# Feed-forward weight products as seven half-size products each (Strassen's scheme), inner width in parts of 6, 8 and 8 tiles

## The chip, the cores and the metric

The kernel runs on one core of a Trainium2 chip. The metric is the time of one execution on the device in microseconds. The names of the engines are those of the profile: PE multiplies matrices (PEld is its weight load), DVE and ACT work on elements from SBUF and PSUM, POOL works on elements in SBUF, SP issues the DMAs. R is the row of reciprocal root mean squares of a normalization, one number per token.

## What is computed

Two transformer blocks, one behind the other, on 512 tokens of width 1024, all in float32. The change concerns the feed-forward part that ends each block:

```python
D_FF = 2816
h = h + mixed @ w_out
hn = rms_norm(h, ffn_norm_g)
h = h + (silu(hn @ w_ffn_gate) * (hn @ w_ffn_up)) @ w_ffn_down
```

Everything else (projections, four kinds of attention, gates, branch products) stays as it is.

## The kernel before

Activations stand transposed: `hT` holds the residual as 8 tiles of 128 features by 512 tokens. Every float32 product is made of three fast ones: a matrix is split into a high part (a rounded copy in the type fp32r) and a low part (what the copy leaves), and PE adds high x high, high x low and low x high in PSUM. ACT makes the high part of the weights (`high`, L605, `stage` to `wh`), DVE the low part (`low`, L904, `wl`), or POOL in the phases named in `POOL_LOW` (L516). The weights of a product are one tile of 128 outputs: 8 or 11 blocks of 128x128, 1024 or 1408 columns in `stage`, in two slots. `product` (L1529) runs over the blocks k and the three parts, 24 or 33 matmuls of 512 tokens each into one bank of `psL`.

The feed-forward part is cut into two halves of the inner width, 11 tiles each (`NFH`): phases gu1a, dn1a, gu1b, dn1b for the first layer and the same with 2. A pair of gu is one tile of gate and one of up. For each pair DVE multiplies both products by R (L1313, L1319), ACT takes the tanh (L790), DVE makes the hidden value (L1317, L1321), ACT and DVE split it (L794, L1323) into `hid`. A pair of dn is two of the 8 output chunks, which DVE adds to `hT` (L1338). ACT and DVE also do the squares and gains of the next normalization beside dn1b and dn2b, and beside `out_project`, the phase before.

The order on each engine is written by hand. Engines meet at semaphores: `w_in` (weights landed), `hi`, `lo`, `mm` (product done), `ev` (PSUM bank read). PE goes on as soon as the low part of the next tile is there and its bank is free:

```python
pe.wait_ge(lo[b], PAIR0[name] + i + 1)
pe.wait_ge(ev[b], PAIR0[name] + i)
```

## Time and profile before

| | us |
|---|---|
| median of 2 runs | 1661.76 (1650.31 to 1673.21) |
| the profiled execution | 1652.3 |
| its span, first to last instruction | 1650.5 |
| PE busy | 1607.5 (97%) |
| DVE busy | 839.7 (51%) |
| ACT busy | 535.2 (32%) |
| POOL busy | 203.8 (12%) |

The span leaves 1.8 us of the execution's time outside. Busy PE is the union of its matmuls, which overlap: the time from the start of one to the start of the next is what a stream of them costs, not the duration of one. For DVE, ACT and POOL the mean duration of one operation is also about what it costs in a queue.

### The profile page before, as it was taken

How to read it: one execution, taken by the hardware profiler on the slowest of the kernel's cores; microseconds unless marked ns; L12 is line 12 of the kernel's file. 1: busy time of each engine (PE TensorE's matmuls, PEld its weight loads, DVE VectorE, ACT ScalarE, POOL GpSimd, SP SyncE). 2: the span in 40 equal slices, each digit the busy share in tenths (PEclk: the TensorE clock that was granted, in tenths of full speed). 3: DMA queues.
4: the chain of work that ended last, by engine and by line, in shares of the span. 5: the costliest groups of instructions: out<-in, count | busy, mean ns of one | idle time of the engine just before them, and what ended most of it. 6: DMA issues, size and time to landing. Idle time of an engine off the chain costs nothing.

```text
span 1650.5 us, 21586 instructions
## 1 busy us (share of the span) xinstructions
PE 1607.5 (97%) x7698; PEld 1273.5 (77%) x7698; DVE 839.7 (51%) x1579; ACT 535.2 (32%) x978; POOL 203.8 (12%) x140
## 2 busy tenths in 40 slices
PE   7899999999999999999999999999999999999997
PEld 6766776777878888888899777677777888888886
DVE  5277796436555533555554382332465554245543
ACT  4123443433322322223321363443333322122232
POOL 2222221003000000000002372221220000000000
PEclk9999999999999999999999999999999999999999
DMA  5832220003333332333232201111133333323331
GB/s 142 204 106 60 57 65 20 1 14 107 90 90 102 99 105 77 89 98 104 81 87 78 62 14 52 52 42 36 51 102 98 94 89 109 94 77 99 95 105 69
DMA packets 250508, 132.62 MB, mean 80 GB/s; under 512 B 20938, under 2 KB 247366, under 8 KB 250447
## 3 DMA queue, kind: packets, MB, share of 16 engines
q1 hardware_dynamic: 248318, 123.92, 26.5%
q0 software_dynamic: 2048, 7.77, 1.8%
q8 instruction: 37, 0.61, 0.2%
q14 instruction: 25, 0.20, 0.0%
q10 hardware_dynamic: 80, 0.14, 0.0%
HBM read 129.67 MB, written 6.38 MB: 82 GB/s over the span
## 4 chain that ended last, share of the span: by engine, by line
PE 91%; DVE 5%; DMA 2%; issue 1%; ACT 1%; POOL 0%; SPq 0%; DVEq 0%; ACTq 0%
PE psL L1529 59%; PE psL L1652 12%; PE psS L1529 4%; PE psL L1773 2%; PE psS L1902 2%; PE psT L1663 2%; PE psS L1703 1%; PE psS L1751 1%; DMA stage<-in_w_in 1%; PE psS L1717 1%; PE psL L1868 1%; PE psS L1885 1%; DMA xin<-in_x 1%; DVE W L1158 1%; PE psT L1666 1%
## 5 line engine op out<-in xcount | busy, mean ns | idle before, releaser
L1529 PE MATMUL psL<-hn,wh 128*128 128x512 f32 x1664 | 525.4, 397 | 5.2 <-POOL wl L516 5.0
L1529 PEld LDWEIGHTS psL<-hn,wh 128*128 128x128 f32 x1664 | 313.1, 189 | 82.6 <-POOL wl L516 5.2
L605 ACT ACTIVATE wh<-stage 128x1024 fp32r<-128x1024 f32 (+3 forms) x234 | 239.8, 1025 | 308.8 <-PE psL L1529 199.4
L1529 PE MATMUL psL<-hn,wl 128*128 128x512 f32 x832 | 329.8, 396 | 0.0
L904 DVE TENSOR_TENSOR wl<-stage,wh 128x1024 fp32r<-128x1024 f32 (+1 forms) x152 | 198.8, 1308 | 95.2 <-ACT wh L605 90.3
L1529 PE MATMUL psL<-hid,wh 128*128 128x512 f32 x704 | 221.3, 395 | 0.0
L516 POOL TENSOR_TENSOR wl<-stage,wh 128x1024 fp32r<-128x1024 f32 (+2 forms) x82 | 156.1, 1904 | 522.6 <-ACT wh L605 522.6
L1529 PEld LDWEIGHTS psL<-hn,wl 128*128 128x128 f32 x832 | 156.8, 188 | 36.5
L1652 PE MATMUL psL<-hn,wh 128*128 128x512 f32 x512 | 173.0, 419 | 0.0
L1529 PEld LDWEIGHTS psL<-hid,wh 128*128 128x128 f32 x704 | 132.3, 188 | 32.0
L1529 PE MATMUL psL<-hid,wl 128*128 128x512 f32 x352 | 139.2, 396 | 0.0
L1652 PEld LDWEIGHTS psL<-hn,wh 128*128 128x128 f32 x512 | 87.4, 189 | 35.7 <-issue 22.1
L1652 PE MATMUL psL<-hn,wl 128*128 128x512 f32 x256 | 101.1, 395 | 0.0
L794 ACT ACTIVATE hid<-ft 128x512 f32 (+1 forms) x44 | 27.8, 632 | 208.6 <-DVE ft L1321 208.6
L1529 PE MATMUL psS<-hn,wh 128*128 128x264 f32 x448 | 86.3, 294 | 0.7 <-DVE hn L949 0.7
L1529 PE MATMUL psL<-mix,wh 128*128 128x512 f32 x256 | 80.7, 396 | 0.9 <-DVE wl L904 0.9
L1338 DVE TENSOR_TENSOR hT<-hT,psL 128x512 f32 (+1 forms) x32 | 22.0, 688 | 112.5 <-PE psL L1529 112.5
L1529 PEld LDWEIGHTS psL<-hid,wl 128*128 128x128 f32 x352 | 66.1, 188 | 16.0
L1158 DVE CUSTOM_DVE_ANT_0 W3b<-psS,biasW,sinkb 128x272 f32<-128x272 f32 (+1 forms) x32 | 18.1, 567 | 112.1 <-PE psS L1885 82.6
L790 ACT ACTIVATE ft<-ft 128x512 f32<-128x512 f32 x44 | 27.8, 632 | 146.0 <-DVE ft L1313 146.0
L1529 PEld LDWEIGHTS psS<-hn,wh 128*128 128x128 f32 x448 | 71.8, 194 | 2.5 <-issue 1.2
L1529 PE MATMUL psS<-hn,wl 128*128 128x264 f32 x224 | 64.8, 289 | 0.0
(356 smaller groups left out, 2038.0 us busy)
## 6 DMA issues: line engine op xcount, KB each, us to landing
stage<-in_w_in SPq DMA_DIRECT2D x54, 512.0 KB, 3.8
stage<-in_w_ffn_gate SPq DMA_DIRECT2D x22, 512.0 KB, 3.8
stage<-in_w_ffn_up SPq DMA_DIRECT2D x22, 512.0 KB, 3.8
stage<-in_w_ffn_down SPq DMA_DIRECT2D x16, 704.0 KB, 4.5
stage<-in_w_ff_gate SPq DMA_DIRECT2D x22, 512.0 KB, 3.8
stage<-in_w_ff_up SPq DMA_DIRECT2D x22, 512.0 KB, 3.8
stage<-in_w_ff_down SPq DMA_DIRECT2D x16, 704.0 KB, 4.6
stage<-in_w_out SPq DMA_DIRECT2D x16, 512.0 KB, 3.8
```

Source lines behind the costliest of these rows:

```text
L516: pool.tensor_tensor(wl[:, b, 0:n], stage[:, b, 0:n], wh[:, b, 0:n].bitcast(F32), ALU.subtract).then_inc(lo[b], 1)
L605: act.activation(wh[:, b, 0:n], stage[:, b, 0:n], ACT.Copy).then_inc(hi[b], 1)
L790: act.activation(ft[:, 1, :], ft[:, 0, :], ACT.Tanh, scale=0.5).then_inc(t_ok, 1)
L794: act.activation(hid[:, 0, bass.ds(i, 1), :], ft[:, 4, :], ACT.Copy).then_inc(hid_hi, 1)
L904: v.tensor_tensor(wl[:, b, 0:n], stage[:, b, 0:n], wh[:, b, 0:n].bitcast(F32), ALU.subtract).then_inc(lo[b], 1)
L1158: dv.link(v.tensor_tensor_reduce(out=tile, in0=scores, in1=bias, scale=1.0, scalar=least, op0=ALU.add, op1=ALU.max, accum_out=mx[:, col:co ...
L1338: v.tensor_tensor(hT[:, n, :], hT[:, n, :], psL[:, b, :], ALU.add).then_inc(ev[b], 1)
L1529: ins = pe.matmul(dst, w[:, b, k * P:(k + 1) * P], x[:, part, k, c0:c1], start=k + n == 0, stop=k == kc - 1 and n == 2)
L1652: ins = pe.matmul(psL[:, b, :], w[:, b, k * P:(k + 1) * P], hn[:, part_, k, META:], start=k + n == 0, stop=k == KD - 1 and n == 2)
L1663: ins = pe.transpose(psT[:, 0, n * P:(n + 1) * P], tile[:, col:col + P], ident[:])
L1773: ins = pe.matmul(psL[:, 0, 0:P], cn[0:w, c, :], pt, start=n == 0, stop=n == len(parts) - 1)
L1902: ins = pe.matmul(psS[:, 2 * (i % 2) + 1, h * HD:(h + 1) * HD], pt, vbn[0:w, c, h // 4 * HD:h // 4 * HD + HD], start=n == 0, stop=n == len ...
```

## The change

A pair of weight tiles is now one block product by Strassen's scheme (the form with 15 additions). For gate and up: the left factor has two tiles (gate, up) and two halves of the contraction, the right one two halves of the contraction and two halves of the tokens. In place of eight half products there are seven, each with 128 outputs, 256 tokens and 4 blocks of contraction (3 in the down products of the first part): matmuls of 256 columns, 84 (63) per pair. Down products pair two output chunks (0 with 4, and so on, `CHUNKS`).

Weights: POOL makes four sums of the quarters (`ffn_weights`: s3, s2, s4, s1, each of half a tile's columns); ACT makes high parts (`ffn_high`: 0 of one quarter, 1 and 2 of two sums each, 3 of two quarters); DVE makes the low parts (`ffn_low_a`, `ffn_low` 1 and 2, `ffn_low_aa`). They lie in seven slots in `wh`, `whx`, `wl`, `wlx`; `stagex` is a second buffer for a pair of weights.

Right factors: seven blocks per pair of tiles in `xb` (normalized input) and `hb` (hidden values). DVE makes three instructions of sums (`x_sums`), ACT the high parts, DVE the low ones.

Outputs: products 0, 2 and 4 grow in one PSUM bank; ACT copies it after each of them (`pa`, `pu`, `pv`), and PE may start product 2 or 4 only behind the copy before (`f_copy`). DVE adds the copies to products 1, 3, 5 and 6. Product 6 uses product 1's bank, so PE waits for DVE's first right quarter (`f_add`). R is read from PSUM. The low parts of `out1` and `out2` go from DVE to POOL. The inner width is cut in three parts of 6, 8 and 8 tiles.

The core of the diff:

```diff
-POOL_LOW = ("iq1", "aq1", "uq1", "gates1", "br1", "qa2", "qb2", "gates2", "br2")
+POOL_LOW = ("iq1", "aq1", "uq1", "gates1", "br1", "out1", "qa2", "qb2", "gates2", "br2", "out2")
+CHUNKS = [0, 4, 1, 5, 2, 6, 3, 7]
+SUBS = [(0, 6), (6, 8), (14, 8)]
...
+                for pair in layer_pairs(l):
+                    f0, n = SUBS[pair.sub]
+                    if pair.q % NQ >= 2:
+                        sp.wait_ge(faa_lo, pair.q - 1)
...
+            def ffn_weights(pair):
...
+                raw_here(pair)
+                slot_free(pair, 1)
+                pool.tensor_tensor(s3, a11, a21, ALU.subtract).then_inc(f_sum, 1)
+                slot_free(pair, 2)
+                pool.wait_ge(f_sum, 4 * q + 1)
+                pool.tensor_tensor(s2, a22, s3, ALU.subtract).then_inc(f_sum, 1)
+                slot_free(pair, 3)
+                pool.wait_ge(f_sum, 4 * q + 2)
+                pool.tensor_tensor(s4, a12, s2, ALU.subtract).then_inc(f_sum, 1)
+                slot_free(pair, 4)
+                pool.tensor_tensor(s1, a21, a22, ALU.add).then_inc(f_sum, 1)
...
+            def slot_free(pair, j):
+                if not pair.first:
+                    pool.wait_ge(f_prod, 7 * (pair.q - 1) + j + 1)
...
+            def ffn_low(pair, n):
+                v.wait_ge(f_sum, 4 * pair.q + 2 + n)
+                v.wait_ge(f_hi, 4 * pair.q + n + 1)
...
+            def gate_up(pair, head=None):
...
+                if pair.i:
+                    hidden(prev, slice(0, SEQ), 0)
+                ffn_low_aa(pair)
+                if odd:
+                    for n in range(3):
+                        x_sums(build, c, n)
+                    x_low(build, hb, c, 0)
...
+                ffn_low_a(nxt)
+                ffn_low(nxt, 1)
+                right_quarters(pair)
+                if odd:
+                    x_low(build, hb, c, 1)
...
+                ffn_low(nxt, 2)
...
+                upper_left(pair)
...
+                gated(pair, LEFT if pair.last else slice(0, SEQ), 3)
...
+                lower_left(pair)
...
+            def down(pair, after=None):
...
+                right_quarters(pair)
+                if nxt:
+                    ffn_low(nxt, 2)
+                upper_left(pair)
+                scaled_in(pair, o0, 2 * pair.i, 3)
+                lower_left(pair)
+                scaled_in(pair, o1, 2 * pair.i + 1, 4)
...
+                        if j in (2, 4):
+                            pe.wait_ge(f_copy, 3 * q + j // 2)
+                        if j in (3, 5):
...
+                                pe.wait_ge(f_add, 4 * (q - 1) + (2 if j == 3 else 3))
+                        if j == 6:
+                            pe.wait_ge(f_add, 4 * q + 1)
...
+                            for n, (wt, part) in enumerate(((high_slot(j, w), 0), (high_slot(j, w), 1), (low_slot(j, w), 0))):
+                                ins = pe.matmul(z_bank(pair, j), wt[:, c * P:(c + 1) * P], x[:, part, c, BLK[j], :],
```

What stands in a row on DVE before, the last gate/up pair of the first half (`ft` and `hid` are the steps of the hidden value, names in brackets the semaphores):

```order
L904 TENSOR_TENSOR wl<-stage,wh 128x1024 [waits hi1]
L1313 TENSOR_TENSOR ft<-psL,Rk 128x512 [waits mm0]
L904 TENSOR_TENSOR wl<-stage,wh 128x1408 [waits hi0]
L1317 SCALAR_TENSOR_TENSOR ft<-ft 128x512 [waits t_ok]
L1319 TENSOR_TENSOR ft<-psL,Rk 128x512 [waits mm1,dve_own]
L1321 SCALAR_TENSOR_TENSOR ft<-ft 128x512 [waits ev1]
L1323 TENSOR_TENSOR hid<-ft,hid 128x512 [waits hid_hi]
```

And now, the third gate/up pair of the first part, one of those with sums of hidden blocks (`wlx<-wsx,whx` and `wl<-ws,wh` are the lows of the next pair's sums, `ux` and `gx` the up and gate values):

```order
L1560 TENSOR_TENSOR wl<-stagex,wh 128x1024 [waits f_hi]
L1522 TENSOR_TENSOR xq<-xq 128x2x256 [waits xq_ok]
L1525 TENSOR_TENSOR xq<-xq 128x256 [waits x_sum]
L1530 TENSOR_TENSOR xq<-xq 128x256 [waits x_sum]
L1535 TENSOR_TENSOR hb<-xq,hb 128x512 [waits x_hi]
L1554 TENSOR_TENSOR wlx<-stage,whx 128x512 [waits f_hi]
L1549 TENSOR_TENSOR wlx<-wsx,whx 128x1024 [waits f_hi,f_sum]
L1624 TENSOR_TENSOR ux<-pv,psS 128x256 [waits f_copy,xq_ok]
L1625 TENSOR_TENSOR gx<-pv,psL 128x256
L1537 TENSOR_TENSOR hb<-xq,hb 128x1280 [waits x_hi]
L1549 TENSOR_TENSOR wl<-ws,wh 128x1024 [waits f_hi,f_sum]
L1630 TENSOR_TENSOR gx<-pa,psL 128x256 [waits f_prod]
```

The upper left quarter of this pair (L1630) now stands behind the low of the next pair's last two sums (L1549), which waits for ACT and through it for POOL.

ACT before, a gate/up pair of the first half:

```order
L605 ACTIVATE wh<-stage 128x1024 [waits mm1,w_in1]
L790 ACTIVATE ft<-ft 128x512 [waits ev0]
L605 ACTIVATE wh<-stage 128x1408 [waits mm0,w_in0]
L794 ACTIVATE hid<-ft 128x512 [waits hid_ok]
```

ACT now, from the copy behind product 0 of an ordinary pair to that of the next (`psT<-gx` is the tanh):

```order
L1035 ACTIVATE pa<-psS 128x256 [waits f_add,f_prod]
L956 ACTIVATE whx<-stagex 128x512 [waits f_prod,raw_in00]
L1048 ACTIVATE pu<-psS 128x256 [waits f_add,f_prod]
L960 ACTIVATE whx<-wsx 128x1024 [waits f_prod,f_sum]
L1056 ACTIVATE pv<-psS 128x256 [waits f_add,f_prod]
L960 ACTIVATE wh<-ws 128x1024 [waits f_prod,f_sum]
L1022 ACTIVATE psT<-gx 128x512 [waits gx_ok]
L958 ACTIVATE wh<-stagex 128x1024 [waits f_prod,raw_in01,raw_in00]
L1035 ACTIVATE pa<-psS 128x256 [waits f_add,f_prod]
```

The copy that lets PE into product 2 of the next pair (the last row) stands behind the tanh of this pair and the high of the next pair's last two blocks.

## Rows read from the trace of the kernel before

**Rows 1.** The page: busy time of each engine, and the chain by engine.
```profile
PE 1607.5 (97%) x7698; PEld 1273.5 (77%) x7698; DVE 839.7 (51%) x1579; ACT 535.2 (32%) x978; POOL 203.8 (12%) x140
...
PE 91%; DVE 5%; DMA 2%; issue 1%; ACT 1%; POOL 0%; SPq 0%; DVEq 0%; ACTq 0%
```

**Rows 2.** By stage: span, busy (xcount) of PE, PEld, DVE, ACT, POOL; clock, DMA, GB/s.
```profile
467.60:826.00 358.40, 358.38 (x1539) 288.98 (x1540) 175.77 (x199) 102.13 (x124) 0.00 (x0) 1.00 0.33 94
1278.60:1637.00 358.40, 358.37 (x1539) 288.96 (x1540) 165.73 (x190) 96.68 (x115) 0.00 (x0) 1.00 0.31 90
```

**Rows 3.** The chain in order of time: start us, us, what.
```profile
467.62 358.32 PE psL L1529 x1536
...
839.69 49.38 PE psS L1529 x405
```

**Rows 4.** DVE by form: xcount | busy us, mean ns | idle before.
```profile
L904 DVE TENSOR_TENSOR wl<-stage,wh 128x1024 fp32r<-128x1024 f32 x120 | 146.9, 1224 | 72.2 <-ACT wh L605 67.3
L904 DVE TENSOR_TENSOR wl<-stage,wh 128x1408 fp32r<-128x1408 f32 x32 | 51.9, 1623 | 23.0 <-ACT wh L605 23.0
L1321 DVE SCALAR_TENSOR_TENSOR ft<-ft 128x512 f32<-128x512 f32 x44 | 30.5, 692 | 1.5
...
L1252 DVE TENSOR_TENSOR mix<-mix 128x512 f32<-128x512 f32 x16 | 25.1, 1568 | 1.7
...
L1234 DVE COPY lat<-psL 128x128 f32<-128x128 f32 x32 | 9.3, 292 | 34.9 <-PE psL L1773 34.8
...
L1272 DVE SCALAR_TENSOR_TENSOR hn<-hT,gvec,hn x12 | 9.0, 752 | 16.3 <-ACT hn L770 16.3
```

**Rows 5.** ACT by form.
```profile
L605 ACT ACTIVATE wh<-stage 128x1024 fp32r<-128x1024 f32 x166 | 174.2, 1050 | 194.0 <-PE psL L1529 84.7 <-PE psS L1529 69.2 <-PE psL L1652 20.1
...
L790 ACT ACTIVATE ft<-ft 128x512 f32<-128x512 f32 x44 | 27.8, 632 | 146.0 <-DVE ft L1313 146.0
...
L718 ACT ACTIVATE PTb<-psT 128x256 f32<-128x256 f32 x16 | 5.7, 357 | 0.0
```

**Rows 6.** POOL by form.
```profile
L516 POOL TENSOR_TENSOR wl<-stage,wh 128x1024 fp32r<-128x1024 f32 x46 | 110.6, 2406 | 332.6 <-ACT wh L605 332.6
L516 POOL TENSOR_TENSOR wl<-stage,wh 128x512 fp32r<-128x512 f32 x32 | 42.6, 1331 | 172.8 <-ACT wh L605 172.8
...
L516 POOL TENSOR_TENSOR wl<-stage,wh 128x256 fp32r<-128x256 f32 x4 | 2.9, 731 | 17.2 <-ACT wh L605 17.2
```

**Rows 7.** Timeline of branch products 1: start us, us, engine, line.
```profile
375.71 1.29 POOL L516 TENSOR_TENSOR wl<-stage,wh 128x512 fp32r<-128x512 f32 x1 [1.01 <-ACT wh L605]
375.85 1.70 DVE L1252 TENSOR_TENSOR mix<-mix 128x512 f32<-128x512 f32 x1
...
377.67 0.63 ACT L758 ACTIVATE mix<-mix 128x512 f32 x1 [2.04 <-DVE mix L1252]
...
378.21 0.62 ACT L605 ACTIVATE wh<-stage 128x512 fp32r<-128x512 f32 x1
...
378.46 0.69 DVE L1254 TENSOR_TENSOR mix<-mix,mix 128x512 f32 x1 [0.91 <-ACT mix L758]
...
378.90 1.40 POOL L516 TENSOR_TENSOR wl<-stage,wh 128x512 fp32r<-128x512 f32 x1 [1.90 <-ACT wh L605]
379.07 0.68 DVE L1244 SCALAR_TENSOR_TENSOR mix<-gate,psL 128x512 f32<-128x512 f32 x1
```

**Rows 8.** Timeline in the index stage, DVE and POOL.
```profile
96.28 2.40 POOL L516 TENSOR_TENSOR wl<-stage,wh 128x1024 fp32r<-128x1024 f32 x1 [4.63 <-ACT wh L605]
...
96.45 2.58 DVE L1085 TENSOR_TENSOR ikx<-ikn,st 128x320 f32<-128x320 f32 x1
...
99.07 0.49 DVE L1086 TENSOR_TENSOR tmp<-ikx 128x320 f32<-128x320 f32 x1
```

**Rows 9.** Timeline of DVE in gates 1, two operations in a row.
```profile
206.25 0.69 DVE L1141 TENSOR_TENSOR tmp<-psL,Rk 128x512 f32<-128x512 f32 x1
206.85 0.16 DVE L1170 TENSOR_TENSOR st<-st,rsum 128x8 f32<-128x8 f32 x1
```

More of the change, by code:

```diff
@@ L250, in build @@
         assert o <= top[0]
+        spare = keep("spare", [P, 2304])
         hn0 = top[0]
@@ new lines, in build, with scratch, raw, high_slot @@
+        ux2, o = at("ux2", [P, SEQ], o)
+        pa2, o = at("pa2", [P, HALF], o)
+        pu2, o = at("pu2", [P, HALF], o)
+        pv2, o = at("pv2", [P, HALF], o)
+        assert o <= hn0
+        def scratch(pair):
+            return (gx2, ux2, pa2, pu2, pv2) if pair.kind == "dn" and pair.sub == 2 else (gx, ux, pa, pu, pv)
+        def raw(pair, m, part):
+            return (stage if pair.par else stagex)[:, m, part * pair.half:(part + 1) * pair.half]
+        def high_slot(j, width):
+            return whx[:, j, 0:width] if j < 3 else wh[:, (j - 3) // 2, (j - 3) % 2 * SEQ:(j - 3) % 2 * SEQ + width]
@@ L330, in build, with raw_blocks @@
+        def raw_blocks(group):
+            return blocks(xq, tuple(g + (g > 4) for g in group))
         hgf, _ = at("hgf", [P, KD, SEQ], hn0)
@@ L589, in _ @@
             lows("br2")
+            lows("out2")
+            for pair in layer_pairs(2):
+                ffn_weights(pair)
         @block.scalar
@@ L819, in pair1, with ffn_high @@
-            def pair1(i, last):
-                high(name, i, 1)
-                chunk1(i, 0)
-                high_next(name, i, last)
-                chunk1(i, 1)
-            act.wait_ge(mm[1], PAIR0[name])
-            act.activation(hn[:, 0, :, 0:META], metaT[:, 1, :, :], ACT.Copy).then_inc(mhi, 1)
-            with act.Fori(0, PAIRS[name] - 1) as i:
-                pair1(i, False)
-            pair1(PAIRS[name] - 1, True)
+            def ffn_high(pair, n):
+                q, w = pair.q, pair.half
+                if n in (0, 3):
+                    for m in range(1 if n == 0 else 2):
+                        act.wait_ge(raw_in[pair.par][m], 16 * (q // 2 + 1))
+                else:
+                    act.wait_ge(f_sum, 4 * q + 2 * n)
+                if not pair.first:
+                    act.wait_ge(f_prod, 7 * (q - 1) + (1, 3, 5, 7)[n])
+                elif n >= 2:
+                    act.wait_ge(mm[n - 2], PAIR0[f"out{pair.layer}"] + PAIRS[f"out{pair.layer}"])
+                if n == 0:
+                    act.activation(high_slot(0, w), raw(pair, 0, 0), ACT.Copy).then_inc(f_hi, 1)
+                elif n == 3:
+                    act.activation(two_slots(wh, 5, w), (stage if pair.par else stagex)[:, :, w:2 * w], ACT.Copy).then_inc(f_hi, 1)
+                else:
+                    act.activation(two_slots(wh, 2 * n - 1, w), weight_sums(2 * n - 1, w), ACT.Copy).then_inc(f_hi, 1)
@@ L1292, in out_project @@
                 clear_squares()
-                pairs(name, pair)
+                for s in range(KD):
+                    chunk(s)
             def new_rms(ssq_count):
@@ new lines, in ffn, with end_chunk @@
+            def ffn(l, head, start, after):
+                for pair in layer_pairs(l):
+                    if pair.kind == "gu":
+                        gate_up(pair, head if pair.first else None)
+                    else:
+                        if pair.sub == 2 and pair.i == 0:
+                            start()
+                        down(pair, after if pair.sub == 2 else None)
+            branches(1)
+            out_project(1, 0)
+            def end_chunk(s):
+                if s == 0:
+                    meta_low(2)
+                gain_low(CHUNKS[s], s)
+                add_squares(1, s, sqacc[:], tmp[:])
@@ L1372, in _ @@
+            ffn(1, (2, 3), clear_squares, end_chunk)
+            low("kv2", 0, 0)
             low("kv2", 0, 1)
@@ L1508, in _, with product @@
         def _(pe):
-            def product(name, i, b, x, meta=0, made=None, between={}):
+            def product(name, i, b, x, meta=0, made=None, between={}, order=None):
                 pe.wait_ge(lo[b], PAIR0[name] + i + 1)
```

605 lines of the change are left out of this document (421 added, 184 removed).

## The prediction

> **What bounds the kernel now.** I read the page first, then the chain that ended last, then the stages. The page [rows 1] says that PE has work in 97% of the span and DVE in 51%; the chain runs over PE for 91%, and most of it is one line, L1529. The table by stage [rows 2] is for the two feed-forward stretches: in each 358.4 us PE is never idle, DVE has 176 or 166 us of work, ACT 102 or 97, POOL nothing, and the clock is granted in full. The chain [rows 3] holds 1536 matmuls of 512 columns in 358.3 us without a gap: 0.2333 us each. A layer's feed-forward part has 1584 of them (22 gate/up pairs of 48, 8 down chunks of 66), so 369.5 us, and PE alone sets it. Fewer columns would shorten it, if the other three engines keep up.
>
> **What PE gains.** The columns halve and the products go from 8 to 7. A pair is now 7 products of 12 matmuls with 256 columns (9 in the down pairs of the first part, whose inner width is 6 tiles). That is 22 x 84 + 4 x (63 + 84 + 84) = 2772 per layer. The nearest shape is 264 columns, 405 of them in 49.38 us [rows 3], 0.1219 each; through it and 0.2333 at 512 columns, 256 come to 0.1183. So PE alone would need 328.0 us per layer, 41.5 less, 83 in both. A pair would take 9.94 us, a product 1.42, against 11.2 for a pair before.
>
> A rule of the Trainium skill (TensorE: Matmul & The Clock Gate, "Back-to-back issue gap") puts the gap of matmuls at columns / 2.4 + 2.5 ns; the rows contradict it, 233.3 ns where it says 215.8. By it the 2772 would take 302.7 us, another 25 less per layer. The rows decide, and below PE hardly matters.
>
> **What the other engines now do, for one gate/up pair.** Durations from [rows 4]: a DVE operation takes 0.69 us for 512 elements and 1.22 for 1024; 256 lies between 0.29 (128) and 0.69, so 0.43; 1280 between 1.22 and 1.62 (1408), so 1.49. ACT [rows 5]: 0.63, 1.05, and 0.36 for a copy of 256 from PSUM. POOL [rows 6]: 256 elements took 0.73 and an undisturbed 512 1.29, so 384 about 1.0.
> DVE: three lows of 1024 and one of 512, 4.35; four quarter sums, 1.72; the gate times R, 0.69; two steps of the hidden values, 1.38: 8.1 us. Every second pair adds sums and lows of the hidden blocks, 0.69 + 0.43 + 0.43 + 0.69 + 1.49 = 3.7. Mean 10.0, against 5.9 before and against PE's 9.94. ACT has some 6.4, POOL four sums, 5.2. DVE's work alone is as long as PE's.
>
> **The loop through four engines.** More decides the order. As the rows of the order show, DVE does the low of the third and fourth weight sums of the next pair ahead of the upper left quarter of this one, and ACT splits the next pair's last two blocks between the tanh and the copy that product 2 of the next pair waits for. From the start of product 2: three products 4.26, seen 0.2 later; POOL's last sum 0.1 + 1.29; ACT's high 0.1 + 1.05; DVE's low 0.1 + 1.22; quarter 0.43; gate 0.74; tanh 0.1 + 0.63; high of the last blocks 1.05; copy 0.36; 0.1 to PE. Together 11.7 us, and no pair of this kind can be shorter, whatever PE can do. The 0.1 is a mean of the handoffs in [rows 7] (ACT 377.67 after DVE's end at 377.55; POOL 378.90 after ACT's 378.83; DVE 378.46 after ACT's 378.30).
>
> **The port.** [rows 7] show the price of POOL work beside DVE. DVE's subtraction of 512 elements from SBUF and SBUF (L1252) starts 0.14 us after a POOL subtraction, ends 0.55 after POOL's end, and takes 1.70 instead of 0.69. The next one runs first, and POOL's takes 1.40 instead of 1.29. L1244, with one input in PSUM, runs beside POOL's at full speed. [rows 8] show it again: 320 elements (L1085) take 2.58 us beside a POOL operation of 2.40, the next 320 take 0.49. So one blocks the other for its whole length, about 1.15 us for POOL's 512 elements. Before, POOL did nothing in this stage. Now it does four such sums per pair, and they are released by products 1 to 4, just when DVE is at the lows and the hidden sums, all SBUF with SBUF.
> SBUF — State Buffer of the Trainium skill ("The single rule") says that it is an exclusive lock and not a share of bandwidth, between a DVE instruction with two SBUF inputs and a GpSimd one that reads SBUF. The rows above agree. By the rule four sums can cost up to 4.6 us of DVE time per pair; by a shared bandwidth they would cost part of it, which is the first rival.
>
> **Pairs laid out by hand**, with time 0 at the end of the preceding tanh:
> - ordinary: hidden to 1.5, low 2.7, low 3.4; POOL's third sum holds the port until 6.0, so DVE's low of the first two sums ends at 7.1; POOL's last sum, due at 6.2, waits for it and ends at 8.2; high 9.35, low 10.7, quarter 11.1, gate 11.8, tanh 12.5. I take 12.4.
> - with hidden sums: low 2.7, sum 3.4, then POOL's second, third and last sum each stop one DVE operation for 1.1 us, so that the low ends at 8.0, the next two at 8.65 and 9.9. Quarters to 10.7 (PE waits 3 us for them), low of 1280 12.2, low 13.4, quarter 13.9, gate 14.5, tanh 15.3. I take 15.2.
> - last of a part: half the tanh, two hidden sums and three more splits by ACT stand in the same loop: low 11.5, hidden half 12.3, sums 13.5, quarter 13.9, gate 14.3, tanh about 15.0. I take 15.1.
> - first of a part: no gate or tanh of a pair before it, 12.4 - 1.4 = 11.0.
> - down: DVE has 4.35 + 1.72 + four operations for scaling and adding, 2.76: 8.8. With three blocked sums of 1.15: 12.3; I take 12.4. In the first part 7.9 + 3 x 0.87, 10.6; I take 10.7. In the last part DVE also does the squares (and in layer 1 the split for the next stage): 12.8 + 3.45 = 16.2 in layer 1 (1.22 and 0.75 per chunk, twice [rows 4]), 13.7 in layer 2; the very last pair prepares no weights, 9.7 and 7.7.
>
> **The sum.** Per layer 8 ordinary 99.2, 8 with sums 121.6, 3 last 45.3, 3 first 33.0: 299.1. Down: 42.8 + 49.6 + 58.3 = 150.7 in layer 1, 141.2 in layer 2. Together 449.8 and 440.3, against 369.5: 80.3 + 70.8 = 151 slower. At the edges the last product of out_project is followed by the chain residual, gain, sums, split, which fills little of the first pair: about 5 us per layer, an estimate from six DVE and ACT steps of 0.4 to 1.2; bounds 0 (hidden by the first product) and 12. POOL takes over the lows of out_project (2.4 us each [rows 6] against 5.6 per product): nothing, it has 3 us to spare; without that cover 1.2 for each of 8. The loads have the same bytes and go from two buffers; SP waits for DVE's last low two pairs back, some 9 us ahead of need for 3.8 us: nothing. 1652.3 + 151 + 10 = 1813. The median of the two shown runs is 1661.8, 9 above the profiled execution; a measured time may lie higher by that.
>
> The costs that no row shows are how DVE and POOL alternate when both always have work. From one side POOL never blocks DVE (first rival, 1686); from the other every sum costs 1.15 in every pair, also in ordinary ones: 4.6 instead of the 0.7 in mine for 22 ordinary and first pairs in both layers, +86 us, 1899. I stand near the middle because [rows 7] show full blocking, while a third of DVE's work has a PSUM input.
>
> **The rivals.**
> - *No loss at the port.* Loop and DVE work stay: ordinary 11.7, first 10.3, with sums 12.5 (POOL blocks nothing), last 14: 266.5 per layer; down 31.6 + 39.8 + 48.1 or 38.3. Layers 386 and 376.2: +23 + 10, so 1686. For it: DVE's and POOL's phases may settle beside each other. Against: L1252's mean over 16 is 1.57 us [rows 4], which is 14 stopped at 1.69 and 2 free at 0.69. Chance 0.13, within 2%.
> - *PE stays the bound.* DVE steps follow each other 0.61 apart where I count 0.69 [rows 9], so 10.0 of work may be 9.2. If the loop also came below 9.94, PE would run through: 1652.3 - 83 + 10 = 1579, faster. That takes 1.8 us out of the loop, which has only 0.8 in handoffs; it decides if product 2 never waits for the copy. Chance 0.07.
> - *Blocked at every sum*, 1899 at the end. Chance 0.15, slower.
> - The forecast as summed, 1813: 0.65.
>
> **How the numbers follow.** About 2% is what a measurement of this kernel can tell from no change. Slower: 0.65 + 0.15 = 0.80; within 2% 0.13; faster 0.07. The range reaches from the port-free case (1686) to near the fully blocked one: 1690 to 1880.
>
> **What would show it.** Right: PE idle in the feed-forward stretch by 20 to 25%, waiting for DVE's quarter sums (product 6) and ACT's copy (product 2); DVE busy over 85%, with SBUF-only operations of 512 elements at a mean of 1 us or more; POOL at some 5 us per pair; pairs of 12 to 15 us. Wrong: matmuls of 256 columns 0.118 apart without gaps, or DVE's lows at their old 1.22 us although POOL works beside them, or a loop shorter than 11 us.

## The result and the profile after

| | before | after |
|---|---|---|
| median of 2 runs, us | 1661.76 | 1944.24 (1943.16 to 1945.31) |
| ratio | | 1.17 (95%: 1.1352 to 1.2048) |
| the profiled execution, us | 1652.3 | 1945.3 |
| mean granted clock of TensorE | 0.99 | 0.92 |

The changed kernel is slower, as forecast, but by 282 us and not by 161 (151 in the feed-forward parts and 10 at their edges): 1944 lies above the top of the range, 1880. The page of after, its rows of busy time, of the granted clock in 40 slices, and of the chain by engine, beside [rows 1]:

```profile
PE 1671.3 (86%) x10074; PEld 1450.0 (75%) x10074; DVE 1274.2 (66%) x2147; ACT 747.2 (38%) x1390; POOL 639.8 (33%) x428
...
PEclk9989996998888989988889999999988889999888
...
PE 50%; DVE 21%; issue 12%; POOL 11%; ACT 4%; DMA 2%; POOLq 0%; SPq 0%; DVEq 0%; ACTq 0%
```

PE is busy in 86% of a longer span. It has more microseconds of work than before although it has fewer columns to multiply, because the clock is no longer granted in full all the time: the slices of 9 in its row are broken by many of 8. The chain has left PE for half of its length; DVE, POOL and handoffs ("issue") hold the rest.

The table by stage for the two feed-forward stretches of after (same columns as [rows 2]; each begins 11 us ahead of the first feed-forward matmul):

```profile
480.00:978.00 498.00, 393.62 (x2809) 380.64 (x2807) 407.33 (x502) 206.54 (x329) 201.35 (x137) 0.89 0.25 70
1436.00:1935.00 499.00, 396.89 (x2843) 383.58 (x2842) 395.81 (x506) 205.51 (x326) 199.78 (x137) 0.90 0.24 68
```

Against [rows 2], DVE went from 176 us of work in 358 to 407 in 498, and PE from never idle to 21% idle. Between the first and the last feed-forward matmul of block 1 PE is busy for 386 us, where 2772 matmuls at 0.1183 us make 328: the clock of 0.89 is in it.

DVE in the first of these stretches, by form (xcount | busy us, mean ns | idle before):

```profile
L1549 DVE TENSOR_TENSOR wlx<-wsx,whx 128x1024 fp32r<-128x1024 f32 x30 | 54.6, 1818 | 49.4 <-POOL ws L723 49.4
L1549 DVE TENSOR_TENSOR wl<-ws,wh 128x1024 fp32r<-128x1024 f32 x30 | 36.4, 1215 | 9.6 <-ACT wh L960 9.6
L1554 DVE TENSOR_TENSOR wlx<-stagex,whx 128x512 fp32r<-128x512 f32 x15 | 21.8, 1457 | 0.4 <-ACT whx L956 0.4
...
L1625 DVE TENSOR_TENSOR gx<-pv,psL 128x256 f32<-128x256 f32 x34 | 13.9, 409 | 0.0
```

The sum of 1024 elements into `wlx` takes 1818 ns and the one into `wl`, the same subtraction of the same size, 1215, its old price [rows 4]. Of the first, 18 of 30 begin while a POOL sum is under way and take 2.2 us on average; the others take 1.21 to 1.23, even three beside which a POOL sum begins later. The second never has a POOL operation beside it. The addition with an input in PSUM (L1625) pays nothing: four of its 34 run wholly beside a POOL sum and take 0.41 to 0.42 us like the rest. POOL in the same stretch:

```profile
L717 POOL TENSOR_TENSOR wsx<-stagex 128x512 f32<-128x512 f32 x15 | 25.5, 1703 | 104.8 <-PE psS L2194 104.8
...
L723 POOL TENSOR_TENSOR ws<-stagex,wsx 128x512 f32<-128x512 f32 x15 | 21.0, 1401 | 2.4 <-POOL wsx L720 0.4
```

POOL pays as well: its sums of 512 elements took 1.29 undisturbed [rows 7], now 1.40 and 1.70 on average in these two rows.

The waits in the same stretch (us in total, times, longest us):

```profile
PE psS L2194 <- DVE ux L1624: 67.9, 32, 3.7
DVE wlx L1549 <- POOL ws L723: 52.4, 22, 4.1
ACT whx L960 <- POOL wsx L720: 49.9, 32, 2.5
...
PE psS L2194 <- ACT pa L1035: 23.4, 10, 6.2
```

This is the loop of the forecast: PE waits for DVE's right quarter (product 6) and ACT's copy (product 2), DVE waits for POOL's sums, and so does ACT. The timeline of one pair shows why (start us, us, engine, line):

```profile
731.68 1.29 POOL L720 TENSOR_TENSOR wsx<-stagex,wsx 128x512 f32<-128x512 f32 x1
...
731.74 1.78 DVE L1554 TENSOR_TENSOR wlx<-stagex,whx 128x512 fp32r<-128x512 f32 x1
...
734.66 1.27 POOL L725 TENSOR_TENSOR ws<-stagex 128x512 f32<-128x512 f32 x1
...
734.74 2.27 DVE L1549 TENSOR_TENSOR wlx<-wsx,whx 128x1024 fp32r<-128x1024 f32 x1 [1.22 <-POOL ws L723]
...
736.94 0.41 DVE L1624 TENSOR_TENSOR ux<-pv,psS 128x256 f32<-128x256 f32 x1
```

POOL's sum at 731.68 and DVE's low at 731.74 start together; DVE takes 1.78 us for what takes 0.69 and ends 0.55 behind POOL's end, as L1252 did in [rows 7]. At 734.66 and 734.74 it happens again with 1024 elements: 2.27 us instead of 1.22, an end 1.08 us behind POOL's. The quarter sum that PE waits for (L1624) comes behind that.

Where the 293 us between the two profiled executions are, by stage of the trace:

| stage | before | after | difference | forecast |
|---|---|---|---|---|
| up to the branch products, block 1 | | | +17 | 0 |
| branch products and `out_project`, blocks 1, 2 | 91.2, 91.0 | 111.0, 110.9 | +20, +20 | 0 |
| feed-forward, blocks 1, 2 | 371.1, 371.1 | 485.8, 479.9 | +115, +109 | +85, +76 |
| to the next stage's first long product; tail | 13.8, 13.6 | 23.2, 16.2 | +9, +3 | 0 |

The forecast's 5 us per layer at the edges belong to the first pair and stand in the feed-forward row.

The first row is not the change. Its instructions are the same, but PE runs at half clock there for 37.5 us. The same 30 us in after and in one of the experiments below, e8 (which changes nothing in this stage either):

```profile
290.00:320.00 30.00, 30.00 (x106) 23.12 (x105) 8.11 (x35) 7.84 (x32) 0.00 (x0) 0.50 0.00 1
```

```profile
290.00:320.00 30.00, 30.00 (x186) 22.91 (x187) 14.05 (x56) 14.51 (x53) 0.00 (x0) 1.00 0.01 1
```

In both PE is busy throughout, with 106 matmuls in the one and 186 in the other. The traces of after, e1 to e6, e12 and e16 have this stretch, and the branch products begin at 374 to 381 us; those of before, e8, e11 and e13 to e15 don't, and they begin at 363 to 365. The runs of before that stand beside the experiments come in two groups, 1650 to 1654 us at a mean clock of 0.99 and 1666 to 1675 at 0.98 (perhaps by this stretch, but no trace of the longer ones shows it), so the experiments are compared by their stages, and by whole times only where the difference is larger than these 16 us.

### The profile page after: what moved, and what is told of

It reads as the page before. It is cut to its first block, busy times and chain, and to the rows that moved or that the text cites. A ratio compares the mean times of both kernels' runs of the same rounds, so it can differ in the third digit from the quotient of the medians.

```text
span 1943.5 us, 27115 instructions
## 1 busy us (share of the span) xinstructions
PE 1671.3 (86%) x10074; PEld 1450.0 (75%) x10074; DVE 1274.2 (66%) x2147; ACT 747.2 (38%) x1390; POOL 639.8 (33%) x428
## 3 DMA queue, kind: packets, MB, share of 16 engines
q8 instruction: 75, 1.23, 0.3%
## 4 chain that ended last, share of the span: by engine, by line
PE 50%; DVE 21%; issue 12%; POOL 11%; ACT 4%; DMA 2%; POOLq 0%; SPq 0%; DVEq 0%; ACTq 0%
PE psS L2194 12%; PE psL L2012 10%; PE psL L1889 9%; PE psS L1889 4%; POOL wsx L720 3%; POOL ws L723 3%; POOL wsx L717 3%; PE psL L2133 2%; DVE wl L1549 2%; PE psS L2296 2%; PE psL L2194 2%; PE psT L2023 1%; DVE wl L1560 1%; POOL wl L659 1%; DVE xq L1522 1%
## 5 line engine op out<-in xcount | busy, mean ns | idle before, releaser
L2194 PE MATMUL psS<-xb,whx 128*128 128x256 f32 x1056 | 218.5, 308 | 21.9 <-ACT pa L1035 19.1
L2194 PE MATMUL psS<-xb,wh 128*128 128x256 f32 x704 | 151.9, 315 | 88.6 <-DVE ux L1624 88.6
L2194 PEld LDWEIGHTS psS<-xb,whx 128*128 128x128 f32 x1056 | 186.1, 216 | 25.3 <-ACT pa L1035 21.3
L1549 DVE TENSOR_TENSOR wlx<-wsx,whx 128x1024 fp32r<-128x1024 f32 (+1 forms) x68 | 123.4, 1814 | 111.2 <-POOL ws L723 111.2
L2194 PEld LDWEIGHTS psS<-xb,wh 128*128 128x128 f32 x704 | 121.9, 213 | 98.2 <-DVE ux L1624 97.3
L2012 PE MATMUL psL<-hn,wh 128*128 128x512 f32 x512 | 173.0, 419 | 0.0
L2194 PE MATMUL psS<-xb,wlx 128*128 128x256 f32 x528 | 159.4, 302 | 0.0
L2194 PE MATMUL psL<-xb,wh 128*128 128x256 f32 x704 | 132.4, 285 | 0.0
L2012 PEld LDWEIGHTS psL<-hn,wh 128*128 128x128 f32 x512 | 87.4, 190 | 35.7 <-issue 22.1
L2012 PE MATMUL psL<-hn,wl 128*128 128x512 f32 x256 | 101.1, 395 | 0.0
```

The lines of the kernel that those rows point to most:

```text
L1549: v.tensor_tensor(two_slots(wl, 2 * n - 1, w), weight_sums(2 * n - 1, w), two_slots(wh, 2 * n - 1, w).bitcast(F32), ALU.subtract).then_inc ...
L2012: ins = pe.matmul(psL[:, b, :], w[:, b, k * P:(k + 1) * P], hn[:, part_, k, META:], start=k + n == 0, stop=k == KD - 1 and n == 2)
L2194: ins = pe.matmul(z_bank(pair, j), wt[:, c * P:(c + 1) * P], x[:, part, c, BLK[j], :], start=c + n == 0 and j not in (2, 4, 6), stop=c == ...
```

## The experiments

Theory: the excess over the forecast is the port, DVE and POOL stopping each other at the weight sums, more often than I laid out. Rivals: the order of the streams (what stands ahead of the instruction that PE waits for); DVE's sheer amount of work; and, for the stage of `out_project`, POOL's longer low. All measured stages, in us (block 1, block 2; "out" is the branch products and `out_project`). The stages are those of the profiled execution; the time is that of the profiled execution for before and after, the median of four runs for e11, e12, e13, e15 and e16, and a single run for the others. e3, e4, e8, e13 and e16 leave out the weight sums:

| kernel | time | out | feed-forward |
|---|---|---|---|
| before | 1652.3 | 91.2, 91.0 | 371.1, 371.1 |
| after | 1945.3 | 111.0, 110.9 | 485.8, 479.9 |
| e1 | 1930.1 | 101.7, 101.4 | 488.5, 482.2 |
| e2 | 1938.4 | 107.2, 107.1 | 486.3, 482.7 |
| e3 | 1756.4 | 109.2, 110.5 | 395.2, 384.6 |
| e4 | 1756.3 | 110.8, 110.6 | 391.5, 388.0 |
| e5 | 1926.9 | 110.9, 110.7 | 479.8, 473.2 |
| e6 | 1934.8 | 107.5, 107.7 | 485.8, 482.7 |
| e8 | 1709.5 | 110.9, 110.8 | 377.3, 371.2 |
| e11 | 1903.8 | 101.7, 101.5 | 482.1, 472.0 |
| e12 | 1811.6 | 99.3, 99.3 | 433.4, 425.6 |
| e13 | 1687.9 | 99.1, 99.3 | 378.9, 369.0 |
| e14 | 1909.5 | 111.1, 110.6 | 474.5, 469.8 |
| e15 | 1782.5 | 99.3, 99.2 | 426.9, 418.0 |
| e16 | 1676.7 | 99.5, 99.2 | 365.0, 359.0 |

**The port: POOL only writes (e3, e4).** POOL's four sums per pair become writes of a constant, at the same places, with the same waits and signals; the sums themselves are left out. The diff is for one of the four sums in e3, where `fill` is six memsets of a sixth each (four for the inner width of 6 tiles); in e4 it is one `pool.memset`. For 512 elements the six took 0.72 us together and the one 0.53, where a sum took 1.35 to 1.72 on average.

```diff
-                pool.tensor_tensor(s3, a11, a21, ALU.subtract).then_inc(f_sum, 1)
+                fill(s3, 0.37).then_inc(f_sum, 1)
```

> Leaves out the weight sums: POOL writes a constant into each of the four, in six pieces (four where the width is 384), about 1.1 us in all, and reads nothing. Its semaphores stay. If DVE and POOL exclude each other over the whole of a POOL operation that reads SBUF, this ends it: DVE's lows and sums return to 1.22, 0.69 and 0.43, ordinary pairs go from 12.7 to 11.9 (the loop), pairs with hidden sums from 15.5 to 12.6, down pairs of 8 tiles from 12.8 to about 10, and the feed-forward stretch from 487 to about 415 us per layer. If what counts is only the length of POOL's steps in the loop, nothing changes by more than 10 us.

> As the run before, with one write of 512 elements per sum, about 0.55 us. If the loop through the four engines sets the ordinary pairs once the port is free, they shorten by the 0.5 to 0.6 us of one POOL step, to 11.3, and the stretch to about 400 us. If DVE's amount of work sets them, they stay at the value of the run before within 0.2.

Measured 1756.4 and 1756.3. DVE by form in e3, one of these lows beside POOL's six writes, and e3's feed-forward part of block 1:

```profile
L1556 DVE TENSOR_TENSOR wlx<-wsx,whx 128x1024 fp32r<-128x1024 f32 x30 | 36.8, 1227 | 33.6 <-POOL ws L714 32.0 <-ACT whx L967 1.6
L1556 DVE TENSOR_TENSOR wl<-ws,wh 128x1024 fp32r<-128x1024 f32 x30 | 36.7, 1223 | 15.9 <-ACT wh L967 15.9
```

```profile
650.69 1.23 DVE L1556 TENSOR_TENSOR wlx<-wsx,whx 128x1024 fp32r<-128x1024 f32 x1
...
651.35 0.73 POOL L714 MEMSET ws<- 128x85 f32 x6 [0.69 <-PE psS L2201]
```

```profile
490.00:885.00 395.00, 351.47 (x2780) 344.33 (x2779) 317.28 (x494) 202.16 (x321) 92.66 (x760) 0.95 0.31 86
```

POOL is still busy for 93 us of the stretch and writes beside DVE's low, which has its old 1227 ns. DVE's work in this part fell from 400 us (in after) to 317 with not one of its instructions changed, and the stage by 91 and 95 us. So POOL's sums, which read SBUF, stop DVE, and writes don't. Not all of the 186 us need be that: the writes are also 0.6 to 1.0 us shorter than the sums, and e4 shortens them by only 0.2 more (391.5 and 388.0 us against 395.2 and 384.6), which is too little to take POOL's own duration out as a part of it. If every one of a block's 34 pairs gained the 0.57 us between an undisturbed sum and the six writes, that would be 19 us of the 91, an estimate from above.

**Order on DVE (e5), and both together (e8).** DVE's low of the next pair's last two sums goes behind the upper left quarter and the gate step (in down pairs behind the first scaling).

```diff
@@ DVE, gate_up @@
-                ffn_low(nxt, 2)
                 upper_left(pair)
                 gated(pair, LEFT if pair.last else slice(0, SEQ), 3)
+                if not pair.last:
+                    ffn_low(nxt, 2)
```

> Only DVE's order changes: the low part of the next pair's last two weight sums stands behind the upper left quarter and the gate (in down pairs behind the first scaled chunk), not ahead of them. If the loop through POOL's last sum, ACT's high and this low sets the pairs, ordinary ones fall from 12.7 towards 11.5 and the stretch from 486 by 10 to 20 us. If the blocking at the port and DVE's work set them, the blocked time stays and they fall by 0.3 at most.

> POOL writes constants as in the port experiment, and DVE's order as in the low-behind-quarter experiment. The loop then has no POOL or weight step in it. If the loop still sets the ordinary pairs at 10.7 there, they fall to PE's own 9.95 to 10.0; pairs with hidden sums stay at 11.2 to 11.4, as DVE works without a pause in them. If DVE's work sets both, nothing changes.

e5 gains 6 to 7 us per block, less than its first reading forecast (10 to 20), e8 another 18 and 13 over e3. Without the sums and with this order the feed-forward part takes 377 and 371 us, the time of before. From one upper left quarter of DVE to the next an ordinary pair then takes 9.1 to 10.0 us and one with sums 11.2, but PE starts its gate/up pairs (but for the very first) 10.0 to 10.2 us apart, its own 9.94, and the chain of this stretch runs over PE for 82% (26% in after). PE is the bound again there. With the port in place the order is worth little: PE's longest wait, for DVE's right quarter, stays (67.9 us in after, 67.4 in e5), because another low stands ahead of that quarter (L1549 into `wlx`) and it is that one which POOL stops. The low that was moved has no POOL operation beside it in either run.

**`out_project` (e1, e2, e6).** In the profile of after the stage has four gaps of PE:

```profile
PE psL L1889 <- POOL wl L659: 12.8, 4, 3.8
```

```profile
424.00:446.00 22.00, 19.64 (x83) 14.91 (x81) 10.66 (x15) 8.88 (x12) 7.15 (x3) 1.00 0.33 96
446.00:468.00 22.00, 15.31 (x51) 11.99 (x52) 8.51 (x12) 8.46 (x12) 8.39 (x4) 0.78 0.17 49
468.00:490.00 22.00, 18.25 (x64) 14.22 (x64) 8.74 (x11) 7.22 (x10) 10.04 (x6) 0.84 0.43 118
```

The gaps are of 1.8, 3.5, 3.7 and 3.8 us. The clock is full in the first stretch, which has the shortest gap, and below full in the two stretches behind the longer ones. The timeline ahead of one of them:

```profile
443.88 1.27 ACT L969 ACTIVATE xb<-xq 128x1280 fp32r<-128x1280 f32 x1 [1.76 <-DVE xq L1530]
...
445.06 1.04 ACT L783 ACTIVATE wh<-stage 128x1024 fp32r<-128x1024 f32 x1
...
446.18 2.71 POOL L659 TENSOR_TENSOR wl<-stage,wh 128x1024 fp32r<-128x1024 f32 x1 [6.75 <-ACT wh L783]
...
448.94 1.22 PE L1889 MATMUL psL<-mix,wh 128*128 128x512 f32 x2 [3.53 <-POOL wl L659]
```

POOL idles for 6.75 us until ACT's high is there, and that high stood behind ACT's 1.27 us of work on `xb`, which waited for DVE; POOL then takes 2.71 us where DVE took 1.22, and PE has run dry. e1 moves ACT's high up, e2 gives the lows back to DVE, e6 does both.

```diff
@@ e1, ACT @@
+                high(name, 0, 1)
                 for i in range(PAIRS[name]):
-                    high(name, i, 1)
                     chunk(2 * i)
...
                     chunk(2 * i + 1)
                     if i < PAIRS[name] - 1:
+                        high(name, i + 1, 1)
                         x_high(build, xb, i, 0)
@@ e2, DVE; out1 and out2 are taken out of POOL_LOW @@
+                    if s % 2 == 0:
+                        low(name, s // 2, 1)
                     chunk(s)
+                    if s % 2 == 0 and s < KD - 2:
+                        low(name, s // 2 + 1, 0)
```

> In out_project ACT makes the high part of the next product's second slot ahead of the splits of the right factor, not behind them. Changed kernel: 110.7 us from the first branch product to the first feed-forward product, 90.9 before. If this place in ACT's order is the cause, the stretch falls to 91 to 95 us in each layer (some 16 to 20 less), and the total by 32 to 40. If the slower low part on POOL (2.4 us for 1.2 on DVE) is the cause, it falls by less than 5. The rest of the feed-forward part stays as it is.

> The low parts of out1 and out2 go back to DVE, ACT's order stays as in the change. If ACT's order is the cause of the longer out_project, only the step itself gets shorter, 2.7 against 1.2 us, three times per layer: 110.7 falls by 4 to 6. If the low parts on POOL are the cause, it falls to 91 to 95.

> Both edits in out_project together: ACT's high ahead of the splits, and the low parts on DVE. Each alone took 9.4 and 3.8 of the 20 us. If PE's gaps there, 12.8 us in four, and the halved clock behind each are the whole cost, both together leave no gap: 5.6 us per product, a granted clock of 1.0 from first to last product of out1, 92 to 95 us from branch to feed-forward. If the right factor's work on DVE is a bound of its own, it stays over 98.

e1 takes 9.4 us out of the stage in both blocks, half of what its first reading forecast and twice the second, e2 3.8, e6 3.4: together they do worse than e1 alone, and the return to 92 to 95 us that I expected of e6 did not come. In e6 PE waits 12.1 us for DVE's own low (four times, longest 6.0): the low now stands behind DVE's sums for `xb`. ACT's order is half of the 20 us. With POOL's sums gone or on DVE the stage loses another 2.4 us (e11 against e12 and e13). I read from the traces that the rest is the work that the change adds to this stage for `xb`, which makes a low late on either engine; no run tested that.

**What a gap costs (e9).** Before's kernel, with DVE writing a scratch tile three (first block) and four times (second block) ahead of the low of one weight tile, so that PE runs dry once per block in a stream that never stopped. All work is kept.

```diff
+                    if last and name in IDLE:
+                        for _ in range(IDLE[name]):
+                            dv.link(v.memset(ft[:], 0.0))
```

> The kernel before, with DVE kept busy by three (dn1a) or four (dn2a) fills of a free buffer ahead of the last pair's low part, about 2.2 us each, so that PE stands still once per layer, for some 2 and 4 us. If idle time of this length costs clock, the granted clock falls to 0.5 behind the gap, the 512-column matmuls come 0.43 apart for some microseconds, and each gap costs more than its own length, by 2 to 4 us. If not, the matmuls go on 0.233 apart and the feed-forward stretch is longer by the gap alone.

Windows around the gap in the first block (3.1 us), and the timeline of PE behind that in the second:

```profile
624.00:630.00 6.00, 6.00 (x27) 4.70 (x25) 4.80 (x3) 0.03 (x1) 0.00 (x0) 1.00 0.00 0
630.00:636.00 6.00, 2.88 (x10) 2.16 (x9) 5.01 (x4) 1.06 (x1) 0.00 (x0) 0.86 0.21 63
636.00:642.00 6.00, 6.00 (x23) 4.75 (x23) 0.00 (x0) 0.00 (x0) 0.00 (x0) 0.85 0.39 112
642.00:648.00 6.00, 6.00 (x27) 4.88 (x26) 1.92 (x2) 1.06 (x1) 0.00 (x0) 1.00 0.23 66
```

```profile
1454.15 1.22 PE L1533 MATMUL psL<-hid,wh 128*128 128x512 f32 x2 [5.91 <-DVE wl L905]
1455.17 0.63 PE L1533 MATMUL psL<-hid,wl 128*128 128x512 f32 x1
...
1460.56 0.63 PE L1533 MATMUL psL<-hid,wh 128*128 128x512 f32 x2
1461.03 0.40 PE L1533 MATMUL psL<-hid,wl 128*128 128x512 f32 x1
```

Behind the gap of 5.9 us the first 15 matmuls of 512 columns take 6.4 us, from 1454.15 to 1460.56, where at full pitch they take 3.5; then the pitch is 0.233 again (1460.56 to 1461.03 for two). Behind 3.1 us of idleness the first 12 matmuls take 4.45 us instead of 2.8. So these two gaps cost themselves and another 1.7 and 2.9 us at the lower of the two clocks, 1.2 GHz. The feed-forward parts grew by 4.8 and 8.4 us (375.9 and 379.5), and the kernel took 1664.5 us, 12 more than before's profiled execution, with 9 us of idleness put in.

**All work kept, both orders (e11); the sums on DVE (e12); without the sums (e13).** e11 is e1 and e5 together. e12 is e11 with POOL's four sums moved into DVE's row, each behind the wait that released it on POOL; e13 is e11 with the writes of e3.

```diff
@@ e12, DVE, gate_up @@
                 ffn_low_aa(pair)
+                dve_sum(nxt, 0)
+                dve_sum(nxt, 1)
...
                 ffn_low_a(nxt)
+                dve_sum(nxt, 2)
                 ffn_low(nxt, 1)
                 right_quarters(pair)
+                dve_sum(nxt, 3)
```

> The changed kernel with two orders altered and all work kept: ACT writes high(i+1,1) ahead of x_high in out_project (as e1), and DVE's ffn_low(nxt,2) stands behind the upper-left sum (as e5). Theory (time goes to DVE and POOL excluding each other at the weight sums, orders are small): both small gains add, 1944 less 19 (out stage 111 to 102 in both layers) less 13 (feed-forward 486/480 to 480/473) gives about 1912 us, feed-forward still over 470 per layer, slower than the kernel before by 14 to 16%. Rival (order of the streams is the main cause): the two together would bring it under 1800.

> The same two orders, and the weight sums of Strassen's scheme computed by DVE instead of POOL, so that POOL has no work in the feed-forward but the second half of the lows left there. Theory (port exclusion, not DVE's sheer amount of work, is what costs): without the exclusion DVE carries its own 377 per layer of e8 plus the sums at about 1.2 us per 1024-element operation; feed-forward about 430 per layer, the kernel about 1800 us. Rival (POOL's duration itself, or one more operation in DVE's row is as dear as the exclusion): feed-forward stays at 470 or more and the kernel at 1900 or above.

> The same two orders, with POOL's weight sums replaced by writes alone (6 for the inner parts as in e3; the weight sums are left out, the products take whatever the buffers hold). Theory: the bound of this scheme on these engines without the port is 1709 (e8) less 18 (out stage) = 1691 us, so seven products instead of eight, even with sums that disturb nobody, do not get below the kernel before, because DVE and ACT still set the pace of a pair at 9 to 10 us against 8.3 of PE. Rival (PE's bound shows once the others are out of the way): 1600 to 1640 us.

Measured 1903.8 (ratio to before 1.149, 1.140 to 1.157), 1811.6 (1.090, 1.079 to 1.100) and 1687.9 (1.019, 1.010 to 1.027): all three within 12 us of what the theory gave. For e13 the time came out, but not the reason: PE's own pace is 9.94 us per pair and not 8.3, the gate/up pairs stand 10.0 to 10.2 apart on PE, and the chain of the feed-forward part runs over PE for 82%. So without the sums PE sets the regular pairs; what keeps the part at 379 us, above the 328 of its matmuls at full clock, is the first pair (19.7 us), the first down pairs and the last part. The feed-forward stretches of the three:

```profile
465.00:948.00 483.00, 382.90 (x2782) 372.33 (x2782) 408.96 (x498) 205.12 (x323) 190.79 (x132) 0.90 0.26 70
```

```profile
477.00:911.00 434.00, 366.93 (x2782) 357.55 (x2782) 402.17 (x634) 204.09 (x323) 0.00 (x0) 0.92 0.28 78
```

```profile
462.00:841.00 379.00, 350.30 (x2781) 345.25 (x2782) 319.28 (x497) 205.97 (x323) 92.82 (x760) 0.95 0.33 90
```

In e12 POOL has nothing to do and DVE does 634 instructions instead of 498; yet DVE is busy for less time (402 us) than in e11 (409), where POOL did that work for it. DVE by form in e12:

```profile
L1563 DVE TENSOR_TENSOR wlx<-wsx,whx 128x1024 fp32r<-128x1024 f32 x30 | 36.7, 1224 | 1.0
...
L1556 DVE TENSOR_TENSOR wsx<-stage,wsx 128x512 f32<-128x512 f32 x15 | 10.4, 693 | 3.1 <-PE psS L2221 1.7
```

A sum that cost POOL 1.3 to 1.7 us, and DVE another 1.1 of standing still, costs DVE 0.69. "Take it from the busiest engine and give it to the idle one" was the wrong way round here by 92 us (49 and 46 in the feed-forward parts).

**The last part (e14, e15, e16).** e13 left one thing open: in block 1, three pairs of the last part stay at 16.9 to 17.0 us even without port loss. The chain of after shows what sets them (start us, us, what):

```profile
927.55 1.14 DVE sqacc L1515
...
929.41 0.61 ACT tmp L1083
930.02 0.61 ACT tmp L1085
930.63 0.28 ACT pa L1035
930.95 1.71 PE psS L2194 x12
...
932.73 1.46 POOL wsx L720
```

ACT's copy of product 0 (930.63), behind which PE may start product 2 (930.95), stands behind ACT's second lot of squares (929.41, 930.02), and these behind DVE's addition of the first lot (927.55). e14 takes the copy between the two lots, with all the rest of after; e15 is e12 with it, e16 is e13 with it (so it leaves out the weight sums).

```diff
                         after_copy(2 * pair.i)
+                        if nxt and nxt.kind == "dn":
+                            act.wait_ge(f_prod, 7 * nxt.q + 1)
+                            act.wait_ge(f_add, 4 * q + 3)
+                            act.activation(scratch(nxt)[2][:], z_bank(nxt, 0), ACT.Copy).then_inc(f_copy, 1)
                         after_copy(2 * pair.i + 1)
```

> The changed kernel with one order altered: in the last part of each layer, ACT takes the copy of the next pair's first product out of PSUM between the two chunks of squares instead of behind both. All work is kept. Theory (in the last part this copy, and not the port, sets the pair: it stands behind ACT's squares, which wait for DVE's first addition of squares): the three pairs of 16.9, 19.9 and 16.4 us in layer 1 fall to about 13.5, in layer 2 those of 17.7, 16.6 and 13.9 to about 13; about 18 us less, 1925. Rival (the port and DVE's own work set these pairs too): the pairs stay within 1 us of what they were and the time at 1940 or more.

> All work kept: the two orders of e11, the weight sums on DVE as in e12, and the copy ahead of the second chunk's squares. Theory: e12's 1812 less about 3 us for each of the three late pairs in both layers, 1790 to 1795; still slower than the kernel before, since DVE's 400 us of work per layer lie above PE's 328. Rival (the late pairs are DVE's own work now): 1805 or more.

> As e13 (POOL's weight sums replaced by writes alone, so the weight sums are left out), with the copy ahead of the second chunk's squares. Theory: the three pairs of 17.0 us in layer 1 fall to 12.5, where DVE's 12.0 us of work per pair stand, those of 14.5, 13.0 and 14.4 in layer 2 to 12; the halved clock behind the 4.6 us gaps goes as well. About 18 us less than e13: 1670, equal to the kernel before within a per cent. Rival (only the wait moves, DVE's row is the bound): 1683 or more.

e14: the last part's down pairs fall from 67.0 to 56.7 us in block 1 and from 62.4 to 49.9 in block 2, the feed-forward parts by 11.3 and 10.1. In block 1 two of the pairs stay at 16 us, where I expected 13.5. The whole time fell by more, 35 us; the rest is the stage ahead of the branch products, at full clock in this run. e15: 1782.5 us, ratio 1.075 (1.065 to 1.084), the best version that does all the work, still slower than before; it is 8 us below the lower end of what I expected. e16: 1676.7 us, ratio 1.010 (1.001 to 1.020), 7 more than expected. Its feed-forward parts, 365 and 359 us, are the first below before's 371, by 6 and 12 us; `out_project` at 99 us against 91 gives that back. The feed-forward part of e15, block 1:

```profile
463.00:890.00 427.00, 365.30 (x2782) 354.73 (x2782) 401.40 (x632) 203.35 (x323) 0.00 (x0) 0.94 0.28 78
```

DVE is busy for 401 of 427 us, PE for 365, and the chain of this part runs over DVE for 68% and over PE for 7%: with the port out of the way DVE's own work is the bound. No version that does the work beats before.

## Why the prediction was wrong

Pairs are measured here from one upper left quarter of DVE (L1630) to the next. Right were the direction, the loop and most of the pieces:
- PE's price, 1.42 us for a product of 12 matmuls: in the timeline of PE in after, one starts 1.41 behind the one before it where the clock is full (rows below).
- The loop through the four engines, and the waits it would show: PE for DVE's quarters and ACT's copy. Idleness of PE 21%, forecast 20 to 25. DVE was busy in 82 and 80% of the two feed-forward parts, though, where the forecast had over 85.
- The pairs in the middle: ordinary 12.6 on average (forecast 12.4), with hidden sums 15.3 (15.2), down pairs 12.7 to 13.0 and 11.0 (12.4 and 10.7). Part of this is luck. Without the sums (e3) ordinary pairs take 10.8 and those with hidden sums 11.4, where my first rival had 11.7 and 12.5: the work without the port was priced about 1 us too high and the port about 1 us too low, and the two cancel. (Of the 0.9 in ordinary pairs some 0.6 may be e3's shorter POOL step, 0.72 for 1.29, an estimate.)
- The mechanism of the port: DVE's stopped operations of 512 elements end 0.55 us behind POOL's end, as [rows 7] had it. What the Trainium skill says (SBUF — State Buffer, "The single rule"), a lock and not a shared bandwidth, the runs bear out: POOL's writes beside DVE's subtraction cost it nothing (1.23 us in e3), and a sum that POOL began first costs it nearly the sum's whole length (2.27 us for 1.22).

The first matmuls of two products in a row, near the end of the second block's feed-forward part:

```profile
1924.30 0.40 PE L2194 MATMUL psL<-hb,wh 128*128 128x256 f32 x2
...
1925.71 0.40 PE L2194 MATMUL psS<-hb,wh 128*128 128x256 f32 x2
```

Wrong were these steps, 132 us between 1813 and the profiled 1945. The points below sum to 134, because the forecast subtracted 369.5 us per layer where the stage of before takes 371.1.
1. *"POOL takes over the lows of out_project: nothing, it has 3 us to spare."* Measured 20 us per block, 40 in all. I compared POOL's 2.4 us with a product's 5.6 and left out what the low waits for: ACT's high stood behind work on `xb` that the change adds to ACT, and that waits for DVE (e1: 9.4 of the 20; what the rest is was not tested apart). My own fallback, 1.2 us for each of 8, would have given 10 in a block.
2. *"Last of a part 15.1", "first of a part 11.0"* and the first pair of a block, with the 5 us per layer at the edges. Measured 16.0 to 17.4 and 12.8 to 14.2 for the parts of 8, and 22 us for the very first pair against 16. Together 31 us. In e3 the last pairs of the parts of 8 take 14.0 and their first pairs 10.0 to 10.3, so there it is POOL's sums again. In the first pair it is not: from PE's first matmul to that of the next pair it takes 21.6 us in after and still 19.4 and 17.8 in e3. The chain of after runs there over DVE's and ACT's sums and splits of x, the squares and one sum of POOL; that was read and not tested.
3. *The last part's down pairs, 58.3 and 48.8.* Measured 67.0 and 62.4, 22 us in both. I counted DVE's row and not that the copy for the next pair stands behind ACT's squares; with the copy ahead (e14) they take 56.7 and 49.9, within 2 us of the forecast. (The forecast's 16.2 for such a pair is right as a sum, 12.3 and twice 1.22 and 0.75, but it is written there as 12.8 + 3.45.)
4. *The other pairs,* 1 to 5% above the forecast in the mean of their kind: 12 us in both blocks.
5. *Behind the feed-forward parts,* where the forecast had no cost: 9 and 3 us (below).
6. 17 us are not the change's, as shown above.

Two prices inside these points were wrong as well. The port was put at 64 us per block (450 with and 386 without it); e3 is 91 and 95 us shorter than after, which is more than the port alone as said above. In the trace of after 73 and 66 operations of DVE per block took over 0.3 us longer than the shortest of their kind, by 1.04 and 1.03 us on average, so the price of one collision (about 1.15) was near; pairs with hidden sums have mostly four of them, where I laid out three. And the sum had every matmul at 0.1183 us: the feed-forward stretches ran at a clock of 0.89, and both gaps of e9 were followed by matmuls at 1.2 GHz. No row of before could show it in this stage, since PE never stopped there; the forecast should have said so and bounded it. What the clock adds to the time is not shown, because PE is not the bound in after.

The rival "blocked at every sum", 1899, was nearer than the forecast, and even that lacked points 1, 3, 5 and 6. The range's top was drawn below it, when a cost outside the feed-forward part had been put at nothing on a comparison of two durations.

Behind the feed-forward part of block 1 PE stands for 8.5 us, where in before it goes on at once with the next stage:

```profile
977.29 0.28 PE L2194 MATMUL psS<-hb,wl 128*128 128x256 f32 x1
986.07 0.78 PE L1889 MATMUL psS<-hn,wh 128*128 128x264 f32 x2 [8.51 <-issue]
```

The profile names no releaser. In that time DVE and ACT do the last additions, gains and squares, and behind them the next weights' high and low. That is the 9 us of the table; the forecast's edge of 5 us per layer was for the other end, ahead of the first pair.

Not tried: the very first pair of a block with its x work ordered differently, and `out_project` without any x work in it.

## What to carry to other kernels

When a change takes work from the bound engine and gives some to all others, lay out the pair by hand, but then also lay out every place where the pattern is broken: first, last, and the stages before and behind. The regular pairs were right within 5%, in part because two errors cancelled; the irregular ones and the neighbouring stages held nearly all of the error. And an idle engine is no free helper: where two engines lock each other out, the sums that POOL took off DVE cost 92 us more than doing them on DVE (e11 against e12). An operation's own duration says nothing on whether it is in time; ask what its input waits for.
